# A two-layer decoder on one core: the down product of the feed-forward part in two passes, with every third pair of row tiles as seven block products

## The reference

```
def swiglu(h, w_gate, w_up, w_down):
    return (jax.nn.silu(h @ w_gate) * (h @ w_up)) @ w_down
...
        h = rmsnorm(x, ffn_norm[i])
        x = x + swiglu(h, ffn_w_gate[i], ffn_w_up[i], ffn_w_down[i])
```

## Time and profile before

| | |
|---|---|
| median of three runs | 2126.2 us |
| profiled execution, and its span | 2126.86 us, 2124.9 us |
| TensorE busy, matmul records | 2118.8 us (100%), 9859 |
| VectorE busy | 1492.9 us (70%) |
| ScalarE busy | 1195.0 us (56%) |
| moved by DMA, mean rate | 442.35 MB, 208 GB/s |

### The profile page before, as it was taken

The page is one execution under the profiler, slowest core; times in us unless marked ns, Lnnn a source line. Parts: engine busy times, 40 slices in busy tenths (PEclk is TensorE's granted clock), DMA queues, the critical chain, the costliest instruction groups (busy, mean ns, idle before and its releaser), DMA issues.

```text
span 2124.9 us, 28796 instructions
## 1 busy us (share of the span) xinstructions
PE 2118.8 (100%) x9859; PEld 1752.0 (82%) x9859; DVE 1492.9 (70%) x1957; ACT 1195.0 (56%) x1630; POOL 65.6 (3%) x39
## 2 busy tenths in 40 slices
PE   9999999999999999999999999999999999999999
PEld 8888888888888888888888888888888888888887
DVE  5776667788788866555667677776888878855554
ACT  6676657555555554444557576665565555544443
POOL 1111000000000000000011001000000000000000
PEclk9999999999999999999999999999999999999999
DMA  8777457666667675555567778765766666665553
GB/s 279 220 226 208 169 171 219 204 214 204 214 213 221 204 222 191 195 197 191 178 206 233 243 215 256 219 212 188 232 200 215 205 219 207 218 208 198 189 188 136
DMA packets 299740, 442.35 MB, mean 208 GB/s; under 512 B 132528, under 2 KB 135312, under 8 KB 288912
## 3 DMA queue, kind: packets, MB, share of 16 engines
q1 hardware_dynamic: 299248, 441.30, 64.9%
q0 software_dynamic: 320, 0.02, 0.0%
q10 hardware_dynamic: 96, 0.03, 0.0%
HBM read 408.27 MB, written 2.10 MB: 193 GB/s over the span
## 4 chain that ended last, share of the span: by engine, by line
PE 99%; DVE 1%; ACT 0%; issue 0%; DVEq 0%; ACTq 0%
PE acc L1758 16%; PE acc L1760 16%; PE acc L1759 16%; PE work L1758 15%; PE work L1759 15%; PE work L1760 15%; PE work L1908 1%; PE work L1946 1%; PE work L1858 0%; PE work L1919 0%; PE acc L1747 0%; PE work L1953 0%; DVE w_lo L1378 0%; PE work L1922 0%; ACT p_buf L1290 0%
## 5 line engine op out<-in xcount | busy, mean ns | idle before, releaser
L1123 ACT ACTIVATE w_hi<-raw 128x1024 fp32r<-128x1024 f32 x756 | 777.4, 1038 | 600.6 <-PE work L1760 378.1
L1378 DVE TENSOR_TENSOR w_lo<-raw,w_hi 128x1024 fp32r<-128x1024 f32 x756 | 898.0, 1197 | 185.0 <-ACT w_hi L1123 180.0
L1758 PE MATMUL work<-w_hi,xT_hi 128*128 128x512 f32 x1064 | 413.9, 389 | 0.0
L1759 PE MATMUL work<-w_lo,xT_hi 128*128 128x512 f32 x1064 | 413.9, 389 | 0.0
L1760 PE MATMUL work<-w_hi,xT_lo 128*128 128x512 f32 x1064 | 413.9, 389 | 0.0
L1758 PE MATMUL acc<-w_hi,xT_hi 128*128 128x512 f32 (+1 forms) x836 | 325.7, 390 | 0.6 <-DVE w_lo L1378 0.5
L1760 PE MATMUL acc<-w_hi,xT_lo 128*128 128x512 f32 (+1 forms) x836 | 322.2, 385 | 0.0
L1759 PE MATMUL acc<-w_lo,xT_hi 128*128 128x512 f32 (+1 forms) x836 | 322.1, 385 | 0.0
L1759 PEld LDWEIGHTS work<-w_lo,xT_hi 128*128 128x128 f32 x1064 | 199.7, 188 | 41.5
L1758 PEld LDWEIGHTS work<-w_hi,xT_hi 128*128 128x128 f32 x1064 | 199.7, 188 | 41.5
L1760 PEld LDWEIGHTS work<-w_hi,xT_lo 128*128 128x128 f32 x1064 | 199.7, 188 | 41.4
(11 more groups left out here) (176 smaller groups left out, 2418.1 us busy)
## 6 DMA issues: line engine op xcount, KB each, us to landing
raw<-in_ffn_w_down_dram SPq DMA_DIRECT2D x88, 1024.0 KB, 4.8
raw<-in_ffn_w_gate_dram SPq DMA_DIRECT2D x160, 512.0 KB, 3.8
raw<-in_ffn_w_up_dram SPq DMA_DIRECT2D x160, 512.0 KB, 4.7
raw<-in_odd_w_in_dram SPq DMA_DIRECT2D x48, 1024.0 KB, 5.7
raw<-in_even_w_in_dram SPq DMA_DIRECT2D x32, 1024.0 KB, 6.1
raw<-in_even_w_out_dram SPq DMA_DIRECT2D x16, 1024.0 KB, 5.1
raw<-in_odd_w_out_dram SPq DMA_DIRECT2D x16, 1024.0 KB, 6.3
bias<-in_bias_dram SPq DMA_DIRECT2D x24, 384.0 KB, 3.8
```

Of the source, the lines that this page charges most:

```text
L1123: act.activation(w_hi[:, s, 0:out], src, ACT.Copy).then_inc(hi_ready, 1)
L1378: dve.tensor_tensor(w_lo[:, s, 0:out], src, w_hi[:, s, 0:out].bitcast(F32), ALU.subtract).then_inc(lo_ready, 1)
L1758: pe.matmul(out_ps, x_hi, wh, start=start, stop=False)
L1759: pe.matmul(out_ps, x_hi, wl, start=False, stop=False)
```

## The change

The down product is done in two passes of 1024 columns, each over 22 pairs of row tiles (`DOWN_PAIRS`). In a pass a pair is a unit as in gate and up, with two blocks of 512 columns of `w_down` in the place of gate and up, so each chunk is loaded as two transfers of 512 KB. `DOWN_SEVENS` names the seven units: pairs 6, 9, 12, 15, 18 and 21 of the first pass, 7, 10, 13, 16 and 18 of the second; the rest are eights, and the last pair of the second is cut by columns ("last"). The weights' sums and splits are made as in gate and up. The forms are new for each seven: four 128 x 128 operations of VectorE on `hT` (`make_forms`), then `form_high` on ScalarE and `form_low` on VectorE, 128 x 512. Row tiles are staged in pairs, 128 x 512, in a ring of two that lies in `xT_hi` and `xT_lo`: `stage_high` in a pair's first step, `stage_low` at the end of its second, both for the next pair.

The last gate and up chunk now has its two sevens as well; it is mixed in the first eight steps of the first pass. The first pass is mixed in the first nine steps of the second, the second pass's sevens by `mix_last` after pair 18. The hidden words of the last chunk are made at pair 5 and merged at pair 9. In layer 0 the first two transposes of x stand in steps 10 and 12 of the second pass. The down loop is gone: both passes are written out.

```diff
-PARTS = {"seven": ("two", "one", "sums_a", "sums_b"), "eight": ("pair", "pair")}
+PARTS = {"seven": ("two", "one", "sums_a", "sums_b"), "eight": ("pair", "pair"), "last": ("first", "second")}
...
+
+DOWN_PAIRS = 22
+DOWN_SEVENS = ((6, 9, 12, 15, 18, 21), (7, 10, 13, 16, 18))
+DOWN = tuple(tuple("seven" if q in at else "last" if (p, q) == (1, DOWN_PAIRS - 1) else "eight"
+                   for q in range(DOWN_PAIRS)) for p, at in enumerate(DOWN_SEVENS))
+HIDDEN_WORDS, HIDDEN_MERGE = 5, 9
...
+        stage_hi, stage_lo = (t[:, 2 * FIRST_K:2 * FIRST_K + 4, :] for t in (xT_hi, xT_lo))
...
+        down_forms = n_wordsT[:, 0, :, :, :].rearrange("p m t q -> p (m t q)").bitcast(F32).rearrange("p (c q) -> p c q", q=P)
...
+                def units(j, more):
 
                     def middle(i):
                         if i < 3:
-                            make_sums(i, 1, 1 if i == 0 else 0)
+                            make_sums(i, 3, 1 if i == 0 else 0)
...
+                        if i == 3 and not more:
+                            stage_high(0)
+                            stage_low(0)
...
+                def down(p, events):
+
+                    of, sevens, x0 = DOWN[p], DOWN_SEVENS[p], n.x.c
+                    begin = [sum(len(PARTS[v]) for v in of[:q]) for q in range(DOWN_PAIRS)]
+                    kinds = [kind for v in of for kind in PARTS[v]] + AHEAD * ["pair" if p == 0 else "plain"]
+                    for q, what in enumerate(of):
+                        for i in range(len(PARTS[what])):
+                            h = begin[q] + i
...
+                            ahead = dict(hi=kinds[h + AHEAD], lo=kinds[h + AHEAD - 1], staged=(n.kt.c - 1) % 2 if i == 0 else staged, begins=i == 0)
+                            staged = ahead["staged"]
+                            if what == "seven":
+                                half(part=i, layer=layer, first=q == sevens[0], last=q == sevens[-1], closes=closes, **ahead)
+                            elif what == "last":
+                                half(columns=i, **ahead)
+                            else:
+                                half(kt=i, start=(q, i) == (0, 0), held=(q, i) == (0, 0),
+                                     direct_stop=p == 0 and (q, i) == (DOWN_PAIRS - 2, 1), **ahead)
...
+                            if what == "last" and i == 0:
+                                down_residual(2)
+                            events(q, h, h - begin[sevens[-1]] - len(PARTS["seven"]))
+                            for v in sevens:
+                                to = h - begin[v]
+                                if to in (-6, -5, -4):
+                                    e.down_forms(to + 6, v)
+                                if to in (-4, -3, -2):
+                                    since = begin[v] - 1 - max([begin[u] + len(PARTS["seven"]) for u in sevens if u < v], default=0)
+                                    make_sums(to + 4, since, 1 if to == -4 else 0)
+                                if to == -3:
+                                    e.form_high()
+                                if to == -2:
+                                    e.form_low()
+                                    n.form.c += 1
+                            if i < 2 and (p, q) != (1, DOWN_PAIRS - 1):
+                                (stage_high, stage_low)[i]((q + 1) % DOWN_PAIRS)
+
+                def first_pass(q, h, after):
+                    if h < 8:
+                        tail(FB - 2, h)
+                    if (q, h % 2) == (HIDDEN_WORDS, 0):
+                        e.hidden_words()
+                    if q == HIDDEN_MERGE and n.hT.c % FB:
+                        take_hidden(FB - 1)
+
+                def second_pass(q, h, after):
+                    if h < 9:
+                        mix(h, (0, layer))
+                    if layer == 0 and h in (10, 12):
+                        xT(1, h // 2 - 5, n.x.c - 2 + h // 2 - 4, pair=h // 2 - 3)
+                    if 0 <= after < 4:
+                        for i in ((0,), (1,), (2, 3), (4, 5))[after]:
+                            e.mix_last(i)
+                        if after == 3:
+                            n.mix.c += 1
+                            n.sets[0].c += 1
+                            n.sets[1].c += 1
 
...
+                with n.loop(eng, FB - 2, half=len(KINDS), made=len(KINDS), raw=16, up=16, sums=2, mix=1, silu=1, direct=1, sets=(0, 2),
                             hT=1) as j:
...
+                    units(j, True)
+                    body_tail(j)
+                units(FB - 2, False)
+                down(0, first_pass)
+                down(1, second_pass)
+                if layer == 1:
                     down_residual(3)
...
-                def rows(at, tiles=4, start=False):
-                    for t in range(tiles):
-                        half(down=0, stage=t, start=start and t == 0)
-                        if start:
-                            hidden(FB - 1, 2 * t)
-                        stage(at + t + 1, (t + 1) % 4)
-                        half(down=1, stage=t, start=start and t == 0)
-                        if start:
-                            hidden(FB - 1, 2 * t + 1)
-
-                rows(0, start=True)
-                with n.loop(eng, FK // 4 - 2, half=8, made=8, raw=8, kt=4) as j:
-                    rows(j * 4 + 4)
-                rows(FK - 4, tiles=2)
...
+                rest = [(FIRST_K + i, of, 2 * (slice((FB - 1) * NB, FB * NB),), (w_gate, w_up)) for i, of in enumerate(BODY[:FIRST_K])]
+                rest += [(q, of, [slice((2 * p + w) * NB, (2 * p + w + 1) * NB) for w in range(2)], (w_down, w_down))
+                         for p in range(2) for q, of in enumerate(DOWN[p])]
+                parts = [2] * RAW + [len(PARTS[of]) for _, of, _, _ in rest]
+                for i, (k, of, cols, source) in enumerate(rest):
+                    pair_chunk(layer, k, cols, len(PARTS[of]), sum(parts[i:i + RAW]) - 2, source)
+                    if i in (6, FIRST_K + HIDDEN_WORDS + RAW):
                         turn_hidden()
...
+            def stage_high(q):
+
+                n = e.n
+                s = 2 * (n.kt.c % 2)
                 act.wait_ge(hT_ready, n.hT.value())
-                if n.kt.past(4):
-                    act.wait_ge(half_used, n.half.value(-4))
...
-                dve.tensor_tensor(stage_lo[:, t, :], hT[:, bass.ds(kt, 1), :].rearrange("p a b -> p (a b)"),
-                                  stage_hi[:, t, :].bitcast(F32), ALU.subtract).then_inc(slo_ready, 1)
+                dve.tensor_tensor(stage_lo[:, s:s + 2, :], hT[:, 2 * q:2 * q + 2, :],
+                                  stage_hi[:, s:s + 2, :].bitcast(F32), ALU.subtract).then_inc(slo_ready, 1)
...
+            def make_forms(step, q):
+
+                n = e.n
+                made = n.form.value(unit=3)
+                (a0, a1), (b0, b1) = ([hT[:, kt, m * P:(m + 1) * P] for m in range(MT)] for kt in (2 * q, 2 * q + 1))
+                if step == 0:
+                    dve.wait_ge(hT_ready, n.hT.value())
+                    dve.wait_ge(down_flo, n.form.value())
+                    dve.tensor_tensor(down_forms[:, 1, :], a1, b1, ALU.subtract)
+                    dve.tensor_tensor(down_forms[:, 2, :], a0, a1, ALU.subtract).then_inc(down_formed, 1)
+                if step == 1:
+                    dve.wait_ge(down_formed, made + 1)
+                    dve.tensor_tensor(down_forms[:, 3, :], down_forms[:, 2, :], b1, ALU.add).then_inc(down_formed, 1)
+                if step == 2:
+                    dve.wait_ge(down_formed, made + 2)
+                    dve.tensor_tensor(down_forms[:, 0, :], b0, down_forms[:, 3, :], ALU.subtract).then_inc(down_formed, 1)
+
+            def form_low():
+                n = e.n
+                dve.wait_ge(down_fhi, n.form.value(1))
+                dve.tensor_tensor(form_lo[:, n.form.slot(2), :, :], down_forms,
+                                  form_hi[:, n.form.slot(2), :, :].bitcast(F32), ALU.subtract).then_inc(down_flo, 1)
 
...
+                if staged is not None and begins:
+                    pe.wait_ge(slo_ready, n.kt.value())
...
```

More of the change, by code:

```diff
@@ L238, in decoder_kernel @@
     EXTRA = len(KINDS) - 2 * len(BODY)
-    HALVES = 4 + 8 * 8 + 2 * 4 * 8 + 3 * CG * 8 + 2 * (2 * FB * 8 + (FB - 2) * EXTRA + FK * 2)
+    HALVES = 4 + 8 * 8 + 2 * 4 * 8 + 3 * CG * 8 + 2 * (2 * FB * 8 + (FB - 1) * EXTRA
+                                                    + sum(len(PARTS[of]) for half in DOWN for of in half))
+    assert DOWN_PAIRS == FK // 2 and DOWN[0][-1] == "seven" and BODY.index("seven") == 0
     BQ = AQ + 2 * AK
@@ L440, in split_views @@
                 return NB, chunk[:, NB:HALF]
+            if kind in ("first", "second"):
+                at = 1 - ("first", "second").index(kind)
+                return HALF, chunk.rearrange("p (t w n) -> p w t n", t=2, w=2)[:, at, :, :]
             if kind in ("sums_a", "sums_b"):
@@ L447, in split_over @@
```

(29 more changed lines are left out.)

291 lines of the change are left out of this document (146 added, 145 removed).

## The result

The changed kernel takes 2141.8 us (median of 4, 2141.75 to 2142.48) against 2126.2 us: a ratio of 1.0074, 95% interval 1.0058 to 1.0090, so 15.7 us slower. The forecast was 2135.7 us, slower, with a range of 2122 to 2145. The profiled execution took 2141.76 us, 14.9 more than the profiled one of before (2126.86).

The account below looks back on a forecast made before the run. TensorE was taken to bound the kernel nearly throughout. Savings of 18.2 us against waits of 10.8 and 16.9 us in the two layers gave +9.5 us: 2136.4 from the profiled run, 2135.7 from the median, range 2122 to 2145.

Parts of the forecast that it names:

- What goes: TensorE, down product and last gate and up chunk: 78 matmuls fewer at 0.2267 us, 17.7 us saved.
- The `hid` wait, 0.5: TensorE, end of each layer's gate and up: the wait for the hidden words goes, 0.5 us saved.
- VectorE's queue, 10.8 a layer: Down product: stagings stand last in VectorE's queue and come late; TensorE waits, 0.82 us at most places, 10.8 us a layer.
- The transposes, 3.9 and 2.6: Layer 0's second pass, steps 10 and 12: transposes of x ahead of sums and staging, waits of 3.9 and 2.6 us.
- DMA waits at nothing: Weight loads, now in 512 KB halves: no wait on them, 0 us.
- dearer forms: VectorE's 128-wide adds at 0.34 us instead of 0.20: the time is 2145.2 us.
- the span's end: Kernel's end: one add stands behind the last matmul in both kernels, so 0 change.
- 1 (all stagings in time): VectorE's chain to the staging: no staging late, the whole saving comes, 2108.0 us; chance 0.10.
- Rival 2: Down product: smaller waits from cheaper forms, 2130.9 us with forms at 0.13; range 2122 to 2129, chance 0.10.
- Rival 3: VectorE's operations follow without overlap where each waits for a semaphore: near 2155 us; chance 0.10 together with Rival 4.
- Rival 4: Weight loads of the sevens late, VectorE waits in its queue's front: 2146 us; chance 0.10 together with Rival 3.

Follow-up runs that it names:

- experiment 8: Changed kernel with hidden row tiles staged two pairs ahead in a ring of three, and VectorE's transposed-tile subtractions a step later: 2108.5 us, the best version.
- experiments 1: Changed kernel with hidden row tiles staged two pairs ahead instead of one, in a ring of three staged pairs instead of two: 2110.0 us.
- experiment 2: Changed kernel with VectorE's staging subtraction moved within its step, directly behind the weight split, ahead of mixing, sums and forms: 2125.0 us.
- 6: Changed kernel without VectorE's four form additions in 20 of 22 sevens, which reuse the first seven's forms: 2129.9 us.
- 10: experiment 8's kernel with every second pair a seven where possible, three more sevens for each layer than the changed kernel: 2127.0 us.
- 9: experiment 8's kernel with seven and six sevens in the two passes instead of six and five: 2114.2 us.
- 3: Changed kernel with VectorE's part of layer 0's two transposed tiles of x one step later in its queue: 2136.9 us.
- 4: Changed kernel with two added VectorE reductions (16 x 256 and 13 x 256) in layer 1's second pass, steps 11 and 49: 2150.8 us.
- experiment 5: Changed kernel with one added VectorE reduction of 24 x 256 ahead of the staging in step 11 of layer 1's second pass: 2147.8 us.
- 7: Changed kernel with only one seven in each pass (pair 21 of the first, 18 of the second): 2135.2 us.

## Why the prediction was right, and what its size lacked

By its own steps, against the 14.9 us between the profiled executions:

- **What goes**: 78 matmuls, 17.7 us. Right, and experiment 8 shows the whole amount as time.
- **The `hid` wait, 0.5**: the pauses there were 0.39 by matmul starts in each layer, with 0.08 behind each: 0.94. Mis-sized by 0.44 in the change's favour.
- **VectorE's queue, 10.8 a layer**: mechanism and places right. Pauses of 0.81 with 0.08 behind them, 0.89, where I had 0.82: 0.05 from the start of the split (1.35, not 1.30), 0.04 from the released matmul (0.23, not 0.19), less 0.02 in the chain. Layers: 10.7 and 16.3 us of pauses and 1.9 behind them, 28.9 where the sum had 27.7.
- **The transposes, 3.9 and 2.6**: 3.81 and 2.54.
- **DMA waits at nothing**: right. Halves landed in 4.9 us against 4.8 for whole chunks. The Trainium skill (DMA: Bandwidth & Descriptors, section Bandwidth) asks for transfers of 1 MiB or more. Going below that cost no time here: the best version has the same halves and no wait on them.
- **What no step had: the clock.** The prediction took the interval of 0.2267 us, measured at a granted clock of 1.00, for every matmul. Behind the pauses of 3.81 and 2.54 us the granted clock was at its lower level, 1.2 of 2.4 GHz, with 0.427 us a matmul: from 954.03 to 959.29, 12 matmuls take 5.26 us instead of 2.72, 2.54 more with the restart, which the 1.9 don't hold; the eight transposes behind them take 1.07 us to the next matmul (960.36) instead of 0.79, 0.28; from 966.50 to 970.13, nine matmuls take 3.63 instead of 2.04, 1.59. Together 4.4 us. The time still fell inside the range, but its upper end had been drawn for dearer forms: that it had room for the clock was luck.

-17.7 - 0.94 + 28.9 + 4.4 = +14.7 of 14.9. The remaining 0.2 us is the balance of small differences that I did not trace to a cause. One is known: from the last matmul's start to the span's end it is 3.85 us, 0.40 less than before, where the prediction had 0. The forecast from the medians also took off 0.7 us by which before's profiled run stood above its median; the changed kernel's stood on it. 4.4 + 1.2 - 0.44 + 0.2 + 0.7 is the 6.1 us between 2135.7 and 2141.8.

Of the rivals, 1 (all stagings in time) failed by the order, as argued, and experiments 1 and 8 show its 2108.0 to be what a better place in the queue gives: 2108.5. Rival 2 fell with the form at 0.20 us. Rival 3 fell: VectorE's steps kept their overlap (830.70 to 831.30, 0.60 for an operation of 0.69), also behind semaphores. The rule of the Trainium skill, VectorE: DVE Perf Modes, section The DRAIN you can't avoid, that the next operation doesn't start until the pipeline is empty, would have given 0.69, and is not what these rows show; the same paragraph adds that an operation that is not held starts earlier. Rival 4 fell with its loads: no wait of VectorE for a load of weights is in the changed kernel's list of waits.

Shown by experiment: that order, not load or loads, made the pauses (1, 2, 8); the share of the forms (6); that load binds at 110% (10), while at 98% it is not told apart from order (9); that the clock needs no transpose to fall (3, 4, 5, 7), and doesn't fall at the transposes without a pause of 2 us or more (1, 8). Not shown: why the clock falls behind one pause and not behind another of the same length, and where the last 0.2 us come from.

## What to carry to other kernels

Whether an engine at 90% fed another was decided here by where in its queue the awaited operation stood. So walk the queue from the last point at which it cannot run ahead to the operation that is waited for, and compare with the other's work between the same points; then move that operation forward, or make it a turn earlier, before giving up the change. A block product that saves 0.68 us is worth nothing if each instance brings one pause of 0.81. And when pauses of TensorE of 2 us or more are in the forecast, add matmuls at half clock behind them to the upper end: 1.4 to 2.9 us a fall in these profiles.

## What the runs showed of the hardware that I had not expected

- **The granted clock after pauses.** Over the profiles of the changed kernel and the experiments: pauses of TensorE up to 1.87 us never showed a fall; of 12 pauses of 2.0 us, in six kernels, 7 did; of 13 between 2.5 and 5.0 us, 11 did (not one of 2.84 and one of 3.21). Where it fell behind a 2.0 us pause, matmuls had already run again at full rate for 0.2 to 1.1 us. A fall cost 1.4 to 1.7 us; two, at the first pause behind the transposes in the changed kernel and in experiment 5's, were twice as long as the others and cost 2.8 and 2.9, the restart's 0.08 counted in. What decides for the same pause at the same place I can't say from these rows. The Trainium skill, TensorE: Matmul & The Clock Gate, section The HAM clock gate (the "warmup" mystery), gives the clock an idle and a busy level and says that the point of its change differs from run to run of one kernel. That agrees: rows inside a fall show 0.50, and the runs of one kernel spread with it, experiment 2 from 2122.4 (clock 1.0) to 2127.4 (0.998), where experiment 8, without pauses, stays within 0.8 us.
- **Starting again costs 0.08 us** at the matmul after the released one: 1.9 us over the 24 pauses of the changed kernel that end at full clock.
